# The last residual tile in two halves, and another order of gate products, weight splits and output rows in a latent attention

## What is computed

```python
def hybrid_layer(x, ...):                        # run twice, l = 0 and 1
    mod = (c @ w_ada + b_ada)[:, None, :]
    sh_m, sc_m, g_m, sh_f, sc_f, g_f = jnp.split(mod, 6, axis=-1)
    h = rms_norm(x) * (1 + sc_m) + sh_m
    x_lru, q_down, kv_down, k_rope, gate_a, gate_b = jnp.split(h @ w_in, IN_SPLIT_POINTS, axis=-1)
    y_a = rg_lru(causal_depthwise_conv(x_lru, ...), ...)
    y_b = mla(q_down, kv_down, k_rope, ...)      # 8 heads, causal softmax, two heads to a pair
    y = jax.nn.sigmoid(gate_a) * y_a + jax.nn.sigmoid(gate_b) * y_b
    x = x + g_m * (y @ w_out)
    h = rms_norm(x) * (1 + sc_f) + sh_f
    gate, up = jnp.split(h @ w_ffn_in, 2, axis=-1)
    return x + g_f * ((jax.nn.silu(gate) * up) @ w_ffn_out)
# after both layers: return rms_norm(x, final_norm_g)
```

## Time and profile before

| | |
|---|---|
| median of three runs | 2544.63 us (2539.80 to 2549.48) |
| the profiled execution | 2544.61 us |
| its span in the profile | 2542.7 us |
| TensorE, VectorE, scalar engine busy | 2438.3, 1713.2, 992.6 us |
| granted TensorE clock, mean | 0.982 of full |

### The profile page before, as it was taken

The page is one execution under the profiler, slowest core; times in us unless marked ns, Lnnn a source line. Parts: engine busy times, 40 slices in busy tenths (PEclk is TensorE's granted clock), DMA queues, the critical chain, the costliest instruction groups (busy, mean ns, idle before and its releaser), DMA issues.

```text
span 2542.7 us, 27838 instructions
## 1 busy us (share of the span) xinstructions
PE 2438.3 (96%) x10886; PEld 1945.8 (77%) x10886; DVE 1713.2 (67%) x2230; ACT 992.6 (39%) x1330; POOL 162.5 (6%) x234
## 2 busy tenths in 40 slices
PE   6999879999999999999999999999999999999997
PEld 3876338888888888888777778888877777888886
DVE  7876678965667955668987785554699777733334
ACT  4324444422333422434855443222348454422231
POOL 0100240000000000000100000000001000000000
PEclk8999989999999999999999999999999999999999
DMA  7432003555552454553211225554532112223222
GB/s 291 172 129 75 17 17 108 178 190 201 175 205 92 150 189 165 171 170 133 79 58 44 101 82 164 169 191 150 179 111 94 36 46 83 94 80 116 96 82 79
DMA packets 66426, 315.40 MB, mean 124 GB/s; under 512 B 7127, under 2 KB 12631, under 8 KB 45304
## 3 DMA queue, kind: packets, MB, share of 16 engines
q1 hardware_dynamic: 41240, 222.39, 25.3%
q0 software_dynamic: 25056, 91.24, 11.0%
HBM read 311.50 MB, written 2.10 MB: 123 GB/s over the span
## 4 chain that ended last, share of the span: by engine, by line
PE 75%; DVE 14%; ACT 5%; issue 3%; DMA 2%; SPq 0%; POOL 0%; DVEq 0%; ACTq 0%
PE psum L762 21%; PE psum L763 21%; PE psum L764 21%; PE psum L1195 3%; PE psum L930 2%; DVE w_lo L1954 1%; PE psum L1180 1%; PE psum L986 1%; ACT w_hi L1358 1%; DMA big<-in_ada_first 1%; DVE rstd L1797 1%; DVE squares L1843 1%; PE psum L1246 1%; PE psum L1066 1%; DVE x_lo L1838 1%
## 5 line engine op out<-in xcount | busy, mean ns | idle before, releaser
L1954 DVE TENSOR_TENSOR w_lo<-w_raw,w_hi 128x2048 fp32r<-128x2048 f32 (+1 forms) x192 | 418.8, 2181 | 310.5 <-ACT w_hi L1358 307.8
L762 PE MATMUL psum<-x_hi,w_hi 128*128 128x512 f32 x1568 | 618.1, 394 | 7.5 <-DVE w_lo L1954 4.4
L763 PE MATMUL psum<-x_lo,w_hi 128*128 128x512 f32 x1568 | 611.3, 390 | 0.0
L764 PE MATMUL psum<-x_hi,w_lo 128*128 128x512 f32 x1568 | 611.1, 390 | 0.0
L1358 ACT ACTIVATE w_hi<-w_raw 128x2048 fp32r<-128x2048 f32 (+1 forms) x192 | 350.5, 1826 | 494.9 <-DMA w_raw<-in_w 493.8
L763 PE MATMUL psum<-hidden_lo,w_hi 128*128 128x512 f32 x960 | 374.2, 390 | 0.0
L762 PEld LDWEIGHTS psum<-x_hi,w_hi 128*128 128x128 f32 x1568 | 295.1, 188 | 72.3 <-DVE w_lo L1954 6.3
L762 PE MATMUL psum<-hidden_hi,w_hi 128*128 128x512 f32 x896 | 349.1, 390 | 0.0
L764 PE MATMUL psum<-hidden_hi,w_lo 128*128 128x512 f32 x896 | 348.6, 389 | 0.0
L763 PEld LDWEIGHTS psum<-x_lo,w_hi 128*128 128x128 f32 x1568 | 295.2, 188 | 62.3 <-issue 3.1
L764 PEld LDWEIGHTS psum<-x_hi,w_lo 128*128 128x128 f32 x1568 | 294.9, 188 | 61.8
(11 more groups left out here) (473 smaller groups left out, 3419.3 us busy)
## 6 DMA issues: line engine op xcount, KB each, us to landing
w_raw<-in_w SPq DMA_DIRECT2D x160, 1024.0 KB, 4.9
ada_w<-in_ada POOLq DMA_DIRECT2D x168, 512.0 KB, 4.0
w_raw<-in_w SPq DMA_DIRECT2D x32, 704.0 KB, 4.0
big<-in_ada_first SPq DMA_DIRECT2D x12, 768.0 KB, 14.3
big<-in_ada POOLq DMA_DIRECT2D x6, 512.0 KB, 4.6
extra<-in_w_uq SPq DMA_DIRECT2D x8, 384.0 KB, 3.2
residual<-in_xT SPq DMA_DIRECT2D x2, 1024.0 KB, 9.8
cond_row<-in_c_row SPq DMA_DIRECT2D x4, 512.0 KB, 5.6
```

The costliest lines, as they stand in the source:

```text
L762: mm(o, w_h, x_h, start=first, stop=False)
L763: mm(o, w_h, x_l, start=False, stop=False)
L764: return mm(o, w_l, x_h, start=False, stop=last)
L1954: v.tensor_tensor(wl[:, r, 0:n], raw[:, r, 0:n], wh[:, r, 0:n].bitcast(f32), ALU.subtract).then_inc(w_split.sem, 1)
```

## The change

- The last slot (11 products in depth, three each) is made in two halves of 256 positions. The sum of squares, root and reciprocal of the first half run between the second half's products: `last_sums` transposes the sums into columns of 128 positions, the root and the reciprocal are taken on two columns, a diagonal is built and `last_roots` spreads it over the partitions. The final scaling reads it from PSUM, and the stores go in halves, 16 in place of eight.
- `GATE_EARLY` goes from 4 to 6: four gate parts stand between the first projections as before, two more ahead of the first scores, and all others two steps earlier.
- The gate slots' halves: slot 1's high half stays in step 0, its low half is in step 1; the other slots' move to step 2 (scalar) and 3 (VectorE) of each eight. Output slot 1's follow the same pattern (steps 26, 27) in place of behind the last step.
- `proj_lows` comes ahead of `head2_split` in step 1. The first scores wait for two low halves in place of three.
- The first output slot's rows 0 to 5 are in steps 26 to 31; behind them `values2(7)`, row 6, three rows of the second slot, row 7, and the rest of the second slot.
- In the first layer the reciprocal (`first_root`) moves to step 26 and the scaling of the residual (`final_scaled`) to steps 28 to 31 and behind step 31.

```diff
@@ -351,6 +351,15 @@
     return {"up": big[:, 16 + n, :], "gateup": big[:, n, :], "xlru": extra[:, n, :]}[site.st.name]
+last_slot, last_root = len(slots) - 1, cols[:, 16:20]
+HALF = T // 2
+def half_of(half):
+    return slice(HALF * half, HALF * half + HALF)
+def block_of(half, j):
+    return slice(HALF * half + P * j, HALF * half + P * j + P)
@@ -366,7 +375,7 @@
 GATE_STEP = 3 * KD // GATE_PARTS
-GATE_EARLY = 4
+GATE_EARLY = 6
@@ -642,10 +651,11 @@
             load_stage(st)
-    for k in range(KD):
-        eng.wait_ge(S("out_ready").sem, k + 1)
-        load(out[k * P:(k + 1) * P, :], h[:, k, :], "stored")
-    eng.wait_ge(L("stored").sem, 16 * (KD))
+    for half in range(2):
+        for k in range(KD):
+            eng.wait_ge(S("out_ready").sem, KD * half + k + 1)
+            load(out[k * P:(k + 1) * P, half_of(half)], h[:, k, half_of(half)], "stored")
+    eng.wait_ge(L("stored").sem, 16 * 2 * KD)
@@ -778,6 +788,19 @@
                     ins = three(dst, t_h, t_l, wh[:, b, w], wl[:, b, w], k == 0, k == st.kt - 1)
+        elif g == last_slot:
+            for half in range(2):
+                for k in range(st.kt):
+                    if half and k == 4:
+                        last_sums(0)
+                    if half and k == 8:
+                        last_roots(0)
+                    w = slice(k * P, (k + 1) * P)
+                    ins = three(B(2 * r + half, HALF), wh[:, b, w], wl[:, b, w], x_h[:, k, half_of(half)], x_l[:, k, half_of(half)],
+                                k == 0, k == st.kt - 1)
+                if half == 0:
+                    ins.then_inc(S("half_done").sem, 1)
@@ -792,6 +815,23 @@
+    def last_sums(half):
+        eng.wait_ge(sum_added.sem, sum_added.next(me, KD - 2 if half == 0 else 0))
+        eng.wait_ge(S("last_squared").sem, half + 1)
+        for j in range(2):
+            dst, at = ps[:, 4 + half, j:j + 1], block_of(half, j)
+            mm(dst, t1[:, at], ones[:, 0:1], start=True, stop=False)
+            ins = mm(dst, sq[:, (KD - 1) % 2, at], ones[:, 0:1], start=False, stop=True)
+        ins.then_inc(S("last_sums").sem, 1)
+    def last_roots(half):
+        eng.wait_ge(S("last_diag").sem, half + 1)
+        for j in range(2):
+            ins = mm(ps[:, 6 + half, j * P:(j + 1) * P], ones[:], rstd[:, block_of(half, j)], start=True, stop=True)
+        ins.then_inc(S("last_roots").sem, 1)
@@ -1152,7 +1192,7 @@
             if i % 4 == 0:
-                eng.wait_ge(S("proj_low").sem, 4 * (4 * l + pair) + (4 if hd else 2 if pair else 3))
+                eng.wait_ge(S("proj_low").sem, 4 * (4 * l + pair) + (4 if hd else 2))
@@ -1197,18 +1237,22 @@
-        def out_rows(k):
+        def out_rows(s, k):
             st = hybrid[l][4]
-            g = st.slot0
-            if k == 0:
+            g = st.slot0 + s
+            if s == 1 and k == 0:
+                eng.wait_ge(w_split.sem, g + 1)
+                eng.wait_ge(S("exp2").sem, n0 + steps2)
+            if s == 0 and k == 0:
...
                 eng.wait_ge(S("gate_read").sem, KD * (l + 1))
-            next_k(k)
+            if s == 0:
+                next_k(k)
...
                 w = slice((k * st.mt + m) * P, (k * st.mt + m + 1) * P)
-                ins = three(B(m), wh[:, ring_at[g], w], wl[:, ring_at[g], w], head_h[:, k, :], head_l[:, k, :],
+                ins = three(B(2 * s + m), wh[:, ring_at[g], w], wl[:, ring_at[g], w], head_h[:, k, :], head_l[:, k, :],
@@ -1216,14 +1260,15 @@
             proj2(0, o)
-        for n in range(GATE_EARLY):
+        for n in range(GATE_PARTS):
...
             proj2(0, o)
+        for n in range(GATE_PARTS, GATE_EARLY):
+            gate_part(n)
...
         scores2(1)
-        OUT_STEPS = {28: (0,), 29: (1,), 30: (2, 3), 31: (4,)}
@@ -1237,8 +1282,8 @@
                 proj2(pair, late)
-            for k in OUT_STEPS.get(i, ()):
-                out_rows(k)
+            if i + GATE_EARLY >= steps2:
+                out_rows(0, i + GATE_EARLY - steps2)
@@ -1246,14 +1291,18 @@
             ins.then_inc(S("turns2").sem, 1)
-        out_rows(5)
         values2(HEADS2 - 1)
-        out_rows(6)
-        out_rows(7)
-        for s in range(1, hybrid[l][4].slots):
+        out_rows(0, 6)
+        for k in range(3):
+            out_rows(1, k)
+        out_rows(0, 7)
+        for k in range(3, KD):
+            out_rows(1, k)
+        for s in range(2, hybrid[l][4].slots):
...
         mlp(hybrid[l][5:])
-    row_sums()
+    last_sums(1)
+    last_roots(1)
@@ -1318,6 +1367,16 @@
+    def last_part():
+        eng.wait_ge(sum_added.sem, sum_added.seen.get("scalar", 0) + KD - 3)
+        for half in range(2):
+            eng.wait_ge(S("last_added").sem, half + 1)
+            act(sq[:, (KD - 1) % 2, half_of(half)], h[:, KD - 1, half_of(half)], ACT.Square).then_inc(S("last_squared").sem, 1)
+            eng.wait_ge(S("last_sums").sem, half + 1)
+            act(last_root[:, 2 * half:2 * half + 2], ps[:, 4 + half, 0:2], ACT.Sqrt, bias=eps6,
+                scale=1.0 / D).then_inc(S("last_rooted").sem, 1)
@@ -1400,7 +1459,9 @@
                 angle_sine(st, s)
-                if st is section[-1]:
+                if g == last_slot:
+                    last_part()
+                elif st is section[-1]:
@@ -1772,9 +1833,10 @@
                 exps2(n + 2)
-            if i % 8 == 0:
-                split_hi(hybrid[l][3].slot0 + 1 + i // 8)
-        split_hi(hybrid[l][4].slot0 + 1)
+            if i == 0:
+                split_hi(hybrid[l][3].slot0 + 1)
+            if i % 8 == 2:
+                split_hi(hybrid[l][3].slot0 + 2 + i // 8)
@@ -1783,7 +1845,6 @@
         mlp(hybrid[l][5:], None if l else sites[4])
-    root()
@@ -2011,6 +2072,32 @@
+    def last_update(half, bank, gate):
+        if half:
+            eng.wait_ge(slot_done.sem, last_slot + 1)
+        else:
+            eng.wait_ge(S("half_done").sem, 1)
+        x = h[:, KD - 1, half_of(half)]
+        me.count(v.scalar_tensor_tensor(x, B(bank, HALF), gate, x, ALU.mult, ALU.add).then_inc(S("last_added").sem, 1), S("last_added"))
+        eng.wait_ge(*me.own())
+    def last_diag(half):
+        eng.wait_ge(S("last_rooted").sem, half + 1)
+        r = last_root[:, 2 * half:2 * half + 2]
+        me.count(v.reciprocal(r, r).then_inc(me.done.sem, 1), me.done)
+        eng.wait_ge(*me.own())
+        v.tensor_scalar(rstd[:, block_of(half, 0)], ident[:], r[:, 0:1], None, ALU.mult)
+        v.tensor_scalar(rstd[:, block_of(half, 1)], ident[:], r[:, 1:2], None, ALU.mult).then_inc(S("last_diag").sem, 1)
+    def last_scale(half, ks):
+        eng.wait_ge(S("last_roots").sem, half + 1)
+        for k in ks:
+            x = h[:, k, half_of(half)]
+            v.scalar_tensor_tensor(x, x, V("final_norm_g", k), B(6 + half, HALF), ALU.mult, ALU.mult).then_inc(S("out_ready").sem, 1)
@@ -2042,6 +2129,14 @@
                     eng.wait_ge(*me.own())
+                elif g == last_slot:
+                    last_update(0, 2 * r, mods[:, buf, col + s:col + s + 1])
+                    last_diag(0)
+                    last_scale(0, range(0, 4))
+                    last_update(1, 2 * r + 1, mods[:, buf, col + s:col + s + 1])
+                    last_scale(0, range(4, KD))
+                    last_diag(1)
+                    last_scale(1, range(KD))
@@ -2083,11 +2178,6 @@
             split_ahead(st, s)
-            for m in (2 * s, 2 * s + 1):
-                if l == 0:
-                    me.count(v.scalar_tensor_tensor(h[:, m, :], h[:, m, :], V("final_g", m), first_root,
-                                                    ALU.mult, ALU.mult).then_inc(me.done.sem, 1), me.done)
-                    eng.wait_ge(*me.own())
@@ -2584,6 +2674,12 @@
+        def final_scaled(m):
+            me.count(v.scalar_tensor_tensor(h[:, m, :], h[:, m, :], V("final_g", m), first_root,
+                                            ALU.mult, ALU.mult).then_inc(me.done.sem, 1), me.done)
+            eng.wait_ge(*me.own())
@@ -2593,10 +2689,10 @@
         proj_low(0, 1)
+        rope_lows(0)
+        proj_low(0, 3)
         proj_low(0, 2)
-        rope_lows(0)
-        for o in range(3, PROJ_N):
-            proj_low(0, o)
+        proj_low(0, 4)
@@ -2610,12 +2706,13 @@
             if r == 1:
+                if i // 8 + 1 < HEADS2 // 2:
+                    proj_lows(i // 8 + 1)
...
                     head2_split(i // 4 - 1)
-                if i // 8 + 1 < HEADS2 // 2:
-                    proj_lows(i // 8 + 1)
+                else:
+                    split_lo(hybrid[l][3].slot0 + 1)
             if r == 2:
-                split_lo(hybrid[l][3].slot0 + 1 + i // 8)
@@ -2630,14 +2727,20 @@
                 proj_low(pair, now)
+            if r == 3:
+                split_lo(hybrid[l][3].slot0 + 2 + i // 8)
+            if l == 0 and i == 26:
+                eng.wait_ge(S("first_root").sem, 1)
+                me.count(v.reciprocal(first_root, first_root).then_inc(me.done.sem, 1), me.done)
```

(16 more changed lines are left out.)

## The result

The changed kernel takes 2518.91 us, median of four runs (2517.27 to 2519.64), beside 2543.01 us for the kernel before on the same chip: ratio 0.9902, 95% interval 0.989 to 0.9914. The forecast was 2523.0, range 2510 to 2537. Run a second time on another chip it took 2516.38 beside 2543.75, ratio 0.9897 (0.988 to 0.9914). The profiled execution took 2519.19 us with a span of 2517.0.

A forecast was written before the change was run, and what follows sets the result against it. TensorE, busy 2438 of 2543 us, was taken to bound the kernel, so gains are its standstill and low-clock time. The terms sum to -21.3 us, from 2544.6 to 2523.3, said as 2523; range 2510 to 2537.

The forecast's parts named there:

- F: Low-clock windows behind TensorE's waits: of 11.0 us lost, two drops of 1.7 stay, -7.6 us; bounds -11 and 0.
- A: Gate parts 4 and 5 ahead of the first scores: waits of 2.3 and 3.4 us both go, -5.7 us.
- B: Step 2: `proj_w_lo` wait stays at 1.8 us, new 0.9 us wait for slot 1's low weights; +2.4 us.
- C: Steps 10 and 18: four projection waits of 1.7 us go but for 0.1 each, -6.4 us.
- D: End of the heads: 2.1 us of waits a layer go but new ones come, +3.0 us; bounds -2 and +6.
- E: First layer's row sums behind the output projection: 0.8 of the 4.6 us wait stays, -3.8 us; bounds -4.6 and -2.
- G: Last tile in halves: 3.35 us reciprocal replaced by one over two columns, -3.2 us; bounds -6 and 0.
- three signs of being wrong: `extra` or exponentials waits at steps 10 to 12; low-clock windows as long in sum as before; end as long as before.
- rival 2: Gate slots' weights late at steps 10 and 18 too, Scalar stands in rounding: +10 us, 2533; chance 0.10.
- Rival 1: The clock gives nothing back, new gaps draw as many drops as the old: 2530.9 us; chance 0.17.
- rival 3: Wait as long as the load in every eighth step, eight roundings at 5 us: 2563 us; chance 0.03.
- Rival 4: Scalar and VectorE keep ahead at steps 2 and 26 to 31, no clock drop stays: 2514 us; chance 0.10.

The follow-up runs named there:

- experiment 5: Changed kernel with gate parts 4 and 5 behind the first two score products instead of ahead of them: 2523.18 us, ratio 0.9923.
- experiment 7: Changed kernel with gate slot 1's rounding moved from the end of step 0 into the scalar engine's gap before the first scores: 2511.76 us, ratio 0.9873.
- experiment 4: Kernel before with only the gate and output slots' splits moved earlier and `proj_lows` first, four gate parts ahead: 2602.51 us, ratio 1.0232.
- experiment 3: Kernel before with only the first layer's reciprocal moved to step 26 and residual scalings to steps 28 to 31 and behind: 2540.48 us, ratio 0.9991.
- experiment 11: Changed kernel with VectorE waiting for its own write behind each of the 16 final scalings: one run, 2518.70 us.
- experiment 1: Kernel before with only the last slot made in halves (16 stores), attention as before: 2538.36 us, ratio 0.9984.
- experiment 2: Changed kernel with the tail of the kernel before, so the attention's part alone: 2520.07 us, ratio 0.9906.
- experiment 6: Changed kernel with VectorE splitting the head ahead of the low half of the pair's weights in step 1: 2522.54 us, ratio 0.9914.
- experiment 8: Changed kernel with `out_rows(1, 0)` ahead of `values2(7)`, and the reciprocal and all scalings behind step 31, one ahead of the last head's sum: 2517.40 us.
- experiment 10: Changed kernel run again unaltered, in the same rounds as a further improved version: 2516.38 us, ratio 0.9897.

## Why the prediction held, step by step

The direction, the places and nearly all mechanisms were right; the sizes were less so. The terms, each beside what one profiled execution of each kernel gives (F stays an estimate):

| term | forecast | measured |
|---|---|---|
| A gate parts ahead of the first scores | -5.7 | -4.7 |
| B step 2 | +2.4 | +1.4 |
| C steps 10 and 18 | -6.4 | -6.8 |
| D end of the heads | +3.0 | +0.6 |
| E row sums | -3.8 | -4.6 |
| F clock | -7.6 | -11.0 |
| G tail | -3.2 | -4.2 |

They add up to -29.3 beside the 27.9 us of the stretches; the 1.4 us between them is not settled. The likeliest place is F, where I take half of a window's busy time as lost. The start, which no edit touches, gave 2.2 us back, so that the span fell by 25.7. None of my three signs of being wrong came.

*A.* Both waits went (experiment 5 brings back what the two parts had covered). What I missed is the wait of 1.0 us in the second layer: gate part 4 needs the bank that the scalar engine's tanh of tile 0 (L1793) has to read, and that stood behind the rope's roundings. I had counted the two parts as free to start.

*B.* Right in kind: 1.5 for `proj_w_lo` (I took 1.8) and 0.7 for `w_lo` (0.9). The rows of the changed kernel, scalar engine and VectorE:
```profile
1316.16 1.91 ACT L1417 ACTIVATE w_hi<-w_raw 128x2048 fp32r<-128x2048 f32 x1
...
1317.96 1.05 ACT L1712 ACTIVATE proj_w_hi<-extra 128x1024 fp32r<-128x1024 f32 x1
...
1319.11 1.23 DVE L2599 TENSOR_TENSOR proj_w_lo<-extra,proj_w_hi 128x1024 fp32r<-128x1024 f32 x1 [1.69 <-ACT proj_w_hi L1712]
```
It is the scalar engine that is late, as experiment 7 then used.

*C.* Right, and a little more: not 0.1 us is left at steps 10 and 18. The late load of rival 2 did not come: I had put about 1 us of waiting on the scalar engine at steps 10 and 18, and it waited for no load there. Only at step 26 did it, 1.3 and 1.1 us. Experiment 4 shows what happens when the slot is read out too late.

*D.* The places were right, all five of the first layer and both of the second. The sizes were too large: 0.71, 0.24, 0.78, 0.76 and 0.69 us against 1.1, 0.7, 0.85, 0.9 and 0.85; second layer 1.6 against 2.65. For step 27, rows of the changed kernel:
```profile
1418.38 0.29 DVE L2655 TENSOR_REDUCE cols<-psum 128x1 f32<-128x128 f32 x1
1418.70 3.35 DVE L2734 RECIPROCAL small<-small 128x512 f32<-128x512 f32 x1
1422.09 0.16 DVE L2661 RECIPROCAL cols<-cols 128x1 f32<-128x1 f32 x1
...
1422.83 0.66 PE L1291 MATMUL psum<-ident,big 128*128 128x128 f32 x4 [0.71 <-DVE big L2664]
```
The maximum ends at 1418.67, 1.5 us after the slot's load is issued (1417.17 in the same trace). I had taken this distance from the old order (1420.7 to 1422.2), and it held; TensorE's way to step 27's transposes was longer than my 4.4 us, 4.95. And I counted 2.0 a layer as removed where 2.1 went.

*E.* All 4.6 us went (in experiment 3 too, where only the scaling moved). The 0.8 I kept for `cond_row` and the modulation weights had no row behind it.

*F.* This is the term that was mis-sized most. Of the 3.4 us of loss that I expected to stay none stayed: step 2's waits drew no low clock in either layer. The step that was off is the count: by the share that I named (two of six), two places would draw 0.7 of a window, and I put down two. I had also taken step 2's 2.7 us of waiting as one piece; it came as 1.5 and 0.7, with a product between. See the last section for how little luck this needed.

*G.* The step that was off was the price of a final scaling: I took 0.49 us and 0.02 between, and the starts are 0.40 apart, because the new loop does not wait for its own write (experiment 11). The update of the second half then came 0.5 us late and not 1.1, and the last eight took 3.2, not 4.1. But the stores took part of it back. They end 1.0 us behind VectorE where they ended 0.4 behind it before, the 0.7 that the prediction had named for slow stores. From the last product's end to the end it is 10.5 us against my 11.6. What it costs is ahead: 1.9 us more between the row sums and the last product, for which I had 1.7. The rule on many small tiles ("VectorE: DVE Perf Modes", "The TRN2 errata" in the Trainium skill) has each instruction pay a fixed latency. The traces agree where like stands beside like: with the wait in both loops, 16 starts at 0.51 are 8.2 us and eight at 0.784 are 6.3. In the changed kernel 16 starts at 0.40 are 6.4 us, so the wait that was left out won back what the halves cost VectorE.

Rival 1 (2530.9) falls with F, rivals 2 (2533) and 3 (2563) with C. Rival 4 (2514) was nearer than I gave it credit for: all of its clock part came, 2.4 of D's 3.0 us and 1.0 of B's 2.4. The forecast was 4 us high because six of seven terms erred to the same side; with A, which erred to the other, they are 8.0 us off in sum. The start's 2.2 us and the 1.4 us that are not settled hid about half of that, and this part of the hit is luck.

## What to carry to other kernels

Count how many steps lie between the product that reads a weight place out and the rounding that needs its next load. Here the rounding moved six steps ahead made the kernel 2.3% slower by itself (experiment 4), and in the changed kernel, where the products have a lead of two parts more, its waits for loads are gone. So the consumer's lead comes first and the split after it. Look for the gap in which the helper engine waits (2.9 us on the scalar engine, 4.2 on VectorE) and put the work there that is late elsewhere, and then read the next stage's limit: here the output stage would not take more than a part of the time won ahead of it. And leave out a wait for one's own write where nothing that follows reads it; but look at who takes the result, since here the store queue let only 0.2 us of the last 0.9 through.

## What the runs showed that I had not expected

Which wait is followed by a low clock differs. Waits of 1.4 to 1.7 us: the kernel before and experiments 1 and 3 have eight each in the profiled execution, 24, and six were followed by 3.4 us at the low level. They are not spread evenly. The wait of 1.7 us at step 10 was followed by one in five of six cases, the equally long one at step 18 in none of six, the one of 1.5 us at step 2 in one of six, and the last head's of 1.4 us in none of six. The changed kernel and experiments 2, 5, 6, 8, 10 and 11 have two each at step 2 (1.5 us), fourteen, and one was followed by one (experiment 11, second layer). One of six and one of fourteen are not told apart. So of the low clocks behind waits of this length most stood at step 10, whose waits are gone, and the step 2 waits that stayed seldom drew one before. What sets step 10 apart from step 18 no run shows, and pooling the four places, as I did, hides it. The six waits of 3.2 us and more in the first three traces (3.2, 3.4 three times, 4.6 twice) all came with a low clock, of 2.3 us one in three; ahead of the first scores of experiment 5 a wait of 1.6 and one of 2.7 both did. The Trainium skill ("TensorE: Matmul & The Clock Gate", "What's actually happening") has the observation running free of the kernel, which fits a catch that changes from one execution to the next: the kernel before and experiment 1 have the same code in both layers, and in the second one the low clock followed step 2 in the one and step 10 in the other. No run here shows the mechanism itself.

Two scalings of 256 columns with nothing between them overlap by 0.08 us on VectorE: 0.475 us each, a start every 0.40. With a wait for the own write between them they start every 0.51. SP's queue issued the last eight stores of 128 x 256 one behind another in 3.75 us, a start every 0.49, and ended 1.0 us behind the last scaling: it had become the limit of the last microseconds.
